# A mixture-of-experts layer in float32 on one core: the last expert's result is merged with its rows on chip instead of being added to them in memory

## The chip, the core and the metric

The kernel runs on one core of a Trainium2 chip. The metric is the time of one execution on the device, in microseconds (us); lower is better. Five engines work beside each other and wait for one another by semaphores: PE (matrix products; its weight loads are listed as PEld), DVE (vector), ACT (scalar), POOL (GpSimd) and SP (which here only issues DMAs). Each engine takes its instructions strictly in the order of its own program.

## What is computed

One layer of a diffusion backbone for 128 prompt rows and 512 sample rows of 1024 channels: a token-mixing part, then a mixture of 16 experts, then a norm of every row. Prompt and sample rows are routed apart; each expert takes its best 16 prompt rows and 64 sample rows, 80 in all, no row twice within one expert:

```python
cap = EC_CAPACITY * n // N_EXPERTS                 # 16 of 128, 64 of 512
g, idx = lax.top_k(jnp.swapaxes(affin, 1, 2), cap)
xe = jax.vmap(lambda xb, ib: xb[ib])(v, idx)
hdn = jax.nn.silu(jnp.einsum('becd,edf->becf', xe, w_e1)) * jnp.einsum('becd,edf->becf', xe, w_e3)
ye = jnp.einsum('becf,efd->becd', hdn, w_e2) * g[..., None].astype(v.dtype)
out = jax.vmap(lambda ib, yb: jnp.zeros((n, D), yb.dtype).at[ib.reshape(-1)].add(yb.reshape(-1, D)))(idx, ye)
...
x = x + g2 * out                                   # in trunk_layer
y_prompt, y_sample = rmsnorm(x, final_norm_g)      # in reference: the final norm of every row
```

All of it is float32. An expert's weights are 24 MB.

## The kernel before

The order of work on each engine is written out by hand. Up to about 685 us the kernel does token mixing and routing; at its end the 640 rows `x` lie in memory in `acc_dram` and their normed form in `xn_dram`, and the table `idx_t` holds in column e the 80 row numbers of expert e (partitions 0 to 63: sample rows, numbered from 128; 64 to 79: prompt rows).

Then come the 16 experts. The weights of one arrive in twelve chunks of 2 MB, issued by SP (L533 in the loop, L507 for the last expert) into six slots of the buffer `ring`; chunk m goes to slot m mod 6, and the issue waits until the products with the slot's old content are done. A chunk is worked in two halves ("units"): ACT rounds it to a high part `w_hi` (L880), DVE takes the rest (L1307, `ring_lo`, written over the slot), and PE multiplies 80 rows by the parts in 24 products of 80x512 (L1649). Chunks 0 to 7 give the hidden rows, chunks 8 to 11 the output in PSUM. Between chunks 7 and 9 PE turns the hidden rows (L1633) and also the rows of the **next** expert (`turn_xe`, L1627), for which POOL has gathered them by their numbers (L603), DVE modulates them (L1297, L1300), ACT rounds (`hi_xe`, L885) and DVE takes the rest (L1313).

When chunk 11's product is done, DVE multiplies the sums by the gates and `g2` into the tile `ye` (`output`, L1331), and POOL adds the 80 rows of `ye` to `acc_dram` with an indirect DMA that accumulates in memory (L618). PE, POOL and the others run the last expert like the rest, as pass 15 of their loops (ACT, DVE and SP have it written out behind a loop of 15). So a 17th gather, turn, modulation and rounding is done whose result nobody uses.

After the last expert: SP waits for the 16th scatter and loads the 640 rows back from `acc_dram` in five tiles of 128x1024 (`xr`, L539). For each tile ACT squares and sums (L929) and takes a root (L932), DVE scales the sum (L941), takes the reciprocal (L1371) and multiplies the tile by it and by the norm's weights (L1373), and SP stores it to the output (L542):

```python
eng.wait_ge(scattered, 16 * E)                     # SP, before L539
...
eng.wait_ge(fin_loaded[t], 16)                     # ACT, before the Square of tile t
...
eng.scalar_tensor_tensor(out=xr[:, n, :], in0=xr[:, n, :], scalar=rstat[:, 3, n:t], in1=gf,
                         op0=ALU.mult, op1=ALU.mult).then_inc(out_ready, 1)
```

Of the kernel before, what the change touches and what calls it, by code (L numbers as in the profile page):

```python
# [16 lines left out]
P = 128  # L17
D = 1024
KD = D // P
NP, NS = 128, 512  # L20
# [8 lines left out]
E = 16  # L29
# [80 lines left out]
def trunk_layer(nc, a):  # L110
# [18 lines left out]
    with ExitStack() as ctx:  # L129
# [47 lines left out]
        idx_s = sb("idx_s", [CAP, 1], U32)  # L177
        ps = ctx.enter_context(nc.psum_tensor("ps", [P, 8, 512], F32))
# [78 lines left out]
        hs = cu_f[0:CAP, 0:FF]  # L257
        gf = cu_f[:, 2 * D:3 * D]
# [122 lines left out]
        fin_loaded = [sem(f"fin_loaded{t}") for t in range(NT)]  # L381
# [58 lines left out]
        def _(eng):  # L440
# [96 lines left out]
            eng.wait_ge(scattered, 16 * E)  # L537
            for t in range(NT):
                eng.dma_start(xr[:, t, :], acc_dram[P * t:P * t + P, :]).then_inc(fin_loaded[t], 16)  # L539
            for t in range(NT):  # L540
                eng.wait_ge(out_ready, t + 1)
                eng.dma_start(a["y_prompt"][0] if t == 0 else a["y_sample"][0].rearrange("(t p) d -> t p d", p=P)[t - 1],  # L542
                              xr[:, t, :]).then_inc(out_stored, 16)
            eng.wait_ge(out_stored, 16 * NT)
            eng.wait_ge(state_stored, 16)

        @block.gpsimd
        def _(eng):
# [62 lines left out]
            with eng.Fori(0, E) as i:  # L611
                eng.wait_ge(xe_turned, i + 1)
                eng.wait_ge(xe_loaded, i * 16 + 16)
                gather(i + 1)
                step.did(eng.tensor_copy(idx_s[:, :], idx_t[:, bass.ds(i, 1)]))
                step.wait()
                eng.wait_ge(ye_ready, i + 1)
                eng.indirect_dma_start(out=acc_dram, out_offset=bass.IndirectOffsetOnAxis(ap=idx_s[:, 0:1], axis=0),  # L618
                                       in_=ye, in_offset=None, compute_op=ALU.add).then_inc(scattered, 16)
                step.restart()  # L620
                eng.wait_ge(scattered, i * 16 + 16)

        @block.scalar
        def _(eng):
# [272 lines left out]
            def act_expert(i, final):  # L897
                for m in range(2, 12):
                    hi_piece(i, m, (i, m - 2))
                    if m == 3:  # L900
                        swish(i, 0)
                    if m == 7:
                        swish(i, 1)
                        hi_h(i, 0)
                    if m == 10:
                        hi_h(i, 1)
                hi_xe(i + 2)
                if not final:
                    for m in range(2):
                        hi_piece(i + 1, m, (i, m + 10))  # L910
# [13 lines left out]
            for t in range(NT + 1):  # L924
                if t < NT:
                    eng.wait_ge(fin_loaded[t], 16)
                    if t >= 2:
                        eng.wait_ge(fin_ssq, t - 1)
                    eng.activation(xn1[:, t % 2, :], xr[:, t, :], ACT.Square, accum_out=rstat[:, 0, t:t + 1]).then_inc(fin_ssq, 1)  # L929
                if t:  # L930
                    eng.wait_ge(fin_ms, t)
                    eng.activation(rstat[:, 2, t - 1:t], rstat[:, 1, t - 1:t], ACT.Sqrt).then_inc(fin_root, 1)  # L932

        @block.vector
        def _(eng):
# [399 lines left out]
            def dve_expert(i, final):  # L1335
                for m in range(2, 12):
# [7 lines left out]
                    if m == 10:  # L1344
                        split_h(i, 1)
                        modulate_xe(i + 2)
                split_xe(i + 2)
                if not final:
                    for m in range(2):
                        split_piece(i + 1, m)  # L1350
                output(i)
                step.restart()

            split_piece(0, 0)
# [10 lines left out]
            for t in range(NT + 1):  # L1365
                if t < NT:
                    inverse_root(fin_ssq, t + 1, fin_ms, fin_root, t, t + 1)
                if t:
# [4 lines left out]
                    eng.scalar_tensor_tensor(out=xr[:, n, :], in0=xr[:, n, :], scalar=rstat[:, 3, n:t], in1=gf,  # L1373
                                             op0=ALU.mult, op1=ALU.mult).then_inc(out_ready, 1)

        @block.tensor
        def _(eng):
# [262 lines left out]
            with eng.Fori(0, E) as i:  # L1640
# [33 lines left out]
                turn_xe(i + 2)  # L1674
# [3 lines left out]
                hidden_product(11)  # L1678

# [26 lines left out]
```

## Time and profile before

| | |
|---|---|
| time, median of 3 runs | 1800.69 us (1800.22 to 1802.33) |
| the profiled execution's own time | 1802.36 us |
| its span, first to last instruction | 1800.6 us |
| busy: PE, DVE, ACT, POOL | 93%, 78%, 61%, 15% of the span |
| granted TensorE clock, mean | 0.966 |
| read from HBM | 478.91 MB |

The span is what the rows below are counted in; a row's time is from the span's start. A busy share is an average over the whole execution and says nothing of its end. The end must be read in the chain of waits, which goes back from the last instruction to what released it, and in the timelines of the engines beside it. "x72" means that a row merges 72 instructions.

### The profile page before, as it was taken

Reading aid. Unit: us, or ns where it says so; the run is one execution under the profiler, and the core shown is the slowest. Engines: PE = TensorE matmul, PEld = TensorE weight load, DVE = VectorE, ACT = ScalarE, POOL = GpSimd, SP = SyncE. Lnnn points to the kernel's source line nnn. Section 1 sums busy time; section 2 is a strip of 40 time slices with the busy share of each in tenths; the row PEclk is TensorE's granted clock in tenths of the full one; section 3 lists DMA queues with packets and bytes.
Section 4 is the critical chain, followed back from the end, with each engine's and each line's share of the span. In section 5 each row is a group of like instructions: output and inputs, shape, how many; then the busy total and the mean of one; then the engine's idle time right before and its main releaser. Section 6 shows DMA issues by size and latency. Waiting matters only on the chain.

```text
span 1800.6 us, 21011 instructions
## 1 busy us (share of the span) xinstructions
PE 1669.5 (93%) x7966; PEld 1176.8 (65%) x7966; DVE 1399.4 (78%) x1308; ACT 1101.8 (61%) x859; POOL 275.3 (15%) x119
## 2 busy tenths in 40 slices
PE   4698889999999938999999999999999999999994
PEld 0298779778888725666666666666666666666662
DVE  0429999974334567988989989989989989989985
ACT  3325544542522335777777777777777777777773
POOL 2003435510000000002011012022022022022020
PEclk8799999999999968999999999999999999999997
DMA  9821111121325286999999999999999999999983
GB/s 389 312 67 57 39 61 40 50 68 59 96 71 165 104 338 237 362 391 366 378 390 373 376 390 359 389 386 367 386 389 362 383 387 371 381 390 370 379 337 124
DMA packets 142558, 492.49 MB, mean 274 GB/s; under 512 B 11257, under 2 KB 23705, under 8 KB 139456
## 3 DMA queue, kind: packets, MB, share of 16 engines
q1 hardware_dynamic: 137280, 475.75, 70.2%
q0 software_dynamic: 3776, 11.09, 2.8%
q10 hardware_dynamic: 1472, 5.25, 0.8%
q8 instruction: 18, 0.29, 0.1%
q14 instruction: 12, 0.10, 0.0%
HBM read 478.91 MB, written 13.16 MB: 273 GB/s over the span
## 4 chain that ended last, share of the span: by engine, by line
PE 81%; DVE 11%; DMA 5%; issue 1%; ACT 1%; SPq 0%; POOL 0%; DVEq 0%; another core or an unknown queue 0%; ACTq 0%; POOLq 0%
PE ps L1649 59%; PE ps L1493 12%; DVE ring L1076 5%; DMA ring<-in_w_mod 3%; PE ps L1455 2%; PE ps L1555 2%; PE ps L1573 1%; DVE ring L1104 1%; PE ps L1633 1%; DVE a_lo L1010 1%; PE ps L1390 1%; PE ps L1470 1%; DVE ring L1051 1%; PE ps L1627 1%; PE ps L1542 0%
## 5 line engine op out<-in xcount | busy, mean ns | idle before, releaser
L1307 DVE TENSOR_TENSOR ring_lo<-ring,w_hi 128x2048 fp32r<-128x2048 f32 x384 | 872.2, 2289 | 109.6 <-ACT w_hi L880 109.6
L880 ACT ACTIVATE w_hi<-ring 128x2048 fp32r<-128x2048 f32 x384 | 734.9, 1919 | 260.5 <-PE ps L1649 260.4
L1649 PE MATMUL ps<-w_hi,xe_hi 128*80 128x512 f32 x1024 | 402.9, 393 | 3.6 <-DVE xe_lo L1313 3.6
L1649 PE MATMUL ps<-ring_lo,xe_hi 128*80 128x512 f32 x1024 | 402.6, 393 | 0.0
L1649 PE MATMUL ps<-w_hi,xe_lo 128*80 128x512 f32 x1024 | 400.7, 391 | 0.0
L1649 PEld LDWEIGHTS ps<-w_hi,xe_hi 128*80 128x80 f32 x1024 | 151.8, 148 | 87.9 <-issue 4.3
L1649 PEld LDWEIGHTS ps<-w_hi,xe_lo 128*80 128x80 f32 x1024 | 151.7, 148 | 84.2 <-issue 0.5
L618 POOL DMA_INDIRECT acc_dram<-ya,idx_s x16 | 75.3, 4709 | 849.3 <-remote 849.3
L1649 PEld LDWEIGHTS ps<-ring_lo,xe_hi 128*80 128x80 f32 x1024 | 151.7, 148 | 81.0 <-issue 0.5
L1649 PE MATMUL ps<-w_hi,h_hi 128*80 128x512 f32 x512 | 203.1, 397 | 0.0
L1649 PE MATMUL ps<-ring_lo,h_hi 128*80 128x512 f32 x512 | 201.2, 393 | 0.0
L1649 PE MATMUL ps<-w_hi,h_lo 128*80 128x512 f32 x512 | 201.1, 393 | 0.0
L1455 PE MATMUL ps<-u_hi,a_hi 128*128 128x320 f32 x384 | 121.0, 315 | 7.7 <-ACT ring L735 4.1
L1076 DVE SCALAR_TENSOR_TENSOR ring<-ring,cur 128x113 f32<-128x113 f32 (+21 forms) x352 | 122.0, 425 | 0.0
L1455 PE MATMUL ps<-u_hi,a_lo 128*128 128x320 f32 x384 | 120.4, 314 | 0.0
L1455 PE MATMUL ps<-u_lo,a_hi 128*128 128x320 f32 x384 | 120.2, 313 | 0.0
L1026 DVE TENSOR_TENSOR b_lo<-ring,b_hi 128x1024 fp32r<-128x1024 f32 x40 | 49.8, 1256 | 84.1 <-ACT b_hi L697 83.8
L1649 PEld LDWEIGHTS ps<-w_hi,h_lo 128*80 128x80 f32 x512 | 75.8, 148 | 43.7
L697 ACT ACTIVATE b_hi<-ring 128x1024 fp32r<-128x1024 f32 x40 | 41.6, 1055 | 99.8 <-DMA ring<-in_w_in 53.1
L1649 PEld LDWEIGHTS ps<-w_hi,h_hi 128*80 128x80 f32 x512 | 75.7, 148 | 41.0
L1649 PEld LDWEIGHTS ps<-ring_lo,h_hi 128*80 128x80 f32 x512 | 75.7, 148 | 40.8
L594 POOL TENSOR_TENSOR ring<-ring 128x644 f32<-128x644 f32 x16 | 70.4, 4426 | 110.8 <-ACT ring L735 110.8
(234 smaller groups left out, 2048.6 us busy)
## 6 DMA issues: line engine op xcount, KB each, us to landing
ring<-in_w_e SPq DMA_DIRECT2D x192, 2048.0 KB, 10.1
ring<-in_w_mod SPq DMA_DIRECT2D x24, 1024.0 KB, 15.7
ring<-in_w_in SPq DMA_DIRECT2D x12, 1024.0 KB, 5.1
ring<-in_w_in SPq DMA_DIRECT2D x16, 512.0 KB, 3.6
xr<-in_x_sample SPq DMA_DIRECT2D x8, 512.0 KB, 5.8
ring<-in_w_rnn_out SPq DMA_DIRECT2D x8, 512.0 KB, 3.7
ring<-in_w_conv_out SPq DMA_DIRECT2D x8, 512.0 KB, 3.8
ring<-in_w_out SPq DMA_DIRECT2D x8, 512.0 KB, 4.1
```

The costliest lines, as they stand in the source:

```text
L594: eng.tensor_tensor(lr_i[:, t, d, :], lr_i[:, t, d, :], xc[:, t, :], ALU.mult).then_inc(ix_ready, 1)
L618: eng.indirect_dma_start(out=acc_dram, out_offset=bass.IndirectOffsetOnAxis(ap=idx_s[:, 0:1], axis=0), in_=ye, in_offset=None, compute_op= ...
L697: eng.activation(b_hi[q % 4][:, :, :], b_raw[:, q % 4, :, :], ACT.Copy).then_inc(piece_hi, 1)
L880: eng.activation(w_hi[m % 2][:, 2 * half:2 * half + 2, :], chunk(m)[:, 2 * half:2 * half + 2, :], ACT.Copy).then_inc(unit_hi, 1)
L1010: eng.tensor_tensor(a_lo[:, kind, :, :], wa(kind), a_hi[kind % 2][:, :, :].bitcast(F32), ALU.subtract)\
L1026: eng.tensor_tensor(b_lo[:, q % 4, :, :], b_raw[:, q % 4, :, :], b_hi[q % 4][:, :, :].bitcast(F32), ALU.subtract)\
L1076: ins = eng.scalar_tensor_tensor(out=cv[:, t, lo:hi], in0=glu[:, t, lo + s:hi + s], scalar=cur[:, G_CDW + k, t:t + 1], in1=cv[:, t, lo:hi] ...
L1307: eng.tensor_tensor(w_lo(m)[:, 2 * half:2 * half + 2, :], w, w_hi[m % 2][:, 2 * half:2 * half + 2, :].bitcast(F32), ALU.subtract)\
L1455: ins = eng.matmul(ps[:, b + h, 0:HALF], w[:, k, :], x[:, k, HALF * h:HALF * h + HALF], start=k == 0 and part == 0, stop=k == KD - 1 and p ...
L1493: ins = eng.matmul(ps[:, tile_bank(NT * g + t), :], x[:, k, P * t:P * t + P], w, start=k == 0 and n == 0, stop=k == KD - 1 and n == 2)
L1555: ins = eng.matmul(ps[:, tile_bank(NT * 8 + t), :], x[:, k, P * t:P * t + P], w, start=k == 0 and n == 0, stop=k == KD - 1 and n == 2)
L1649: ins = eng.matmul(ps[0:CAP, bank + b, :], x[:, k0 + kk, :], w[:, kk, 512 * b:512 * b + 512], start=first and kk == 0 and n == 0, stop=las ...
```

## The change

1. **The last expert's rows are left out of memory's sum.** POOL's loop is one pass shorter. After it, POOL gathers the 80 rows of expert 15 from `acc_dram` (where the first 15 experts are added up) into `xe`, which is free then. When the expert's `ye` is there, DVE adds `xe` to it; ACT and DVE norm these 80 rows with the same steps as a tile, and POOL writes them to the outputs with two indirect DMAs that don't accumulate: 64 rows to `y_sample`, 16 to `y_prompt`, over what lies there. A small table `idx_out` holds their numbers in each output (one DVE instruction and one small DMA fill it).
2. **The norm of all 640 rows doesn't wait for the last expert.** SP loads the five tiles once 15 scatters have landed and chunks 6 and 7 of the last expert are used up, into `ring` (slots 0 and 1), no longer into `xr`, which still holds `w_hi1`. The squares' unused products go there too. One semaphore counts all five loads, and the first square waits for all of them. The tiles are stored as before. The 80 rows of expert 15 are then stored in an unfinished state, and overwritten: POOL waits for all five stores.
3. **Order.** DVE does the five tiles' norm before `output(15)`. PE's last expert is written out behind a loop of 15. The 17th turn, modulation and rounding are gone.

```diff
@@ buffers @@
+        idx_out = sb("idx_out", [CAP_S, 2], U32)
+        fin = ring[:, 0:NT * D].rearrange("p (t d) -> p t d", t=NT)
+        fin_sq = ring[:, NT * D:(NT + 2) * D].rearrange("p (t d) -> p t d", t=2)
@@ SP @@
                 load_chunk(E - 1, m)
-            eng.wait_ge(scattered, 16 * E)
+            product_done(eng, E - 1, NSLOT)
+            product_done(eng, E - 1, NSLOT + 1)
+            eng.wait_ge(scattered, 16 * (E - 1))
             for t in range(NT):
-                eng.dma_start(xr[:, t, :], acc_dram[P * t:P * t + P, :]).then_inc(fin_loaded[t], 16)
+                eng.dma_start(fin[:, t, :], acc_dram[P * t:P * t + P, :]).then_inc(fin_loaded, 16)
...
             eng.wait_ge(out_stored, 16 * NT)
+            eng.wait_ge(rows_patched, 16 * 2)
@@ POOL @@
-            with eng.Fori(0, E) as i:
+            with eng.Fori(0, E - 1) as i:
...
+            eng.dma_start(idx_out[0:CAP_P, 1:2], idx_t[CAP_S:CAP, E - 1:E]).then_inc(last_prompt_idx, 16)
+            eng.wait_ge(xe_turned, E)
+            eng.indirect_dma_start(out=xe, out_offset=None, in_=acc_dram,
+                                   in_offset=bass.IndirectOffsetOnAxis(ap=idx_t[:, E - 1:E], axis=0)).then_inc(xe_loaded, 16)
+            eng.wait_ge(idx_ready, 4)
+            eng.wait_ge(last_prompt_idx, 16)
+            eng.wait_ge(out_stored, 16 * NT)
+            eng.wait_ge(out_ready, NT + 1)
+            for out, column, lo, hi in ((a["y_sample"][0], 0, 0, CAP_S), (a["y_prompt"][0], 1, CAP_S, CAP)):
+                eng.indirect_dma_start(out=out, out_offset=bass.IndirectOffsetOnAxis(ap=idx_out[0:hi - lo, column:column + 1], axis=0),
+                                       in_=ye[lo:hi, :], in_offset=None).then_inc(rows_patched, 16)
@@ ACT, the last expert and after it @@
-                hi_xe(i + 2)
                 if not final:
+                    hi_xe(i + 2)
...
-                    eng.wait_ge(fin_loaded[t], 16)
+                    eng.wait_ge(fin_loaded, 16 * NT)
...
+            eng.wait_ge(ye_ready, E + 1)
+            eng.wait_ge(out_ready, NT)
+            eng.activation(fin_sq[0:CAP, 1, :], ye, ACT.Square, accum_out=rstat[0:CAP, 0, 0:1]).then_inc(fin_ssq, 1)
+            eng.wait_ge(fin_ms, NT + 1)
+            eng.activation(rstat[0:CAP, 2, 0:1], rstat[0:CAP, 1, 0:1], ACT.Sqrt).then_inc(fin_root, 1)
@@ DVE, the last expert and after it @@
-                        modulate_xe(i + 2)
-                split_xe(i + 2)
+                        if not final:
+                            modulate_xe(i + 2)
                 if not final:
+                    split_xe(i + 2)
                     for m in range(2):
                         split_piece(i + 1, m)
-                output(i)
-                step.restart()
+                    output(i)
+                    step.restart()
+            eng.tensor_scalar(idx_out[:, 0:1], idx_t[0:CAP_S, E - 1:E], float(NP), None, ALU.subtract).then_inc(idx_ready, 1)
...
+            output(E - 1)
+            eng.wait_ge(ye_ready, E)
+            eng.wait_ge(xe_loaded, 16 * (E + 1))
+            eng.tensor_tensor(ye, ye, xe, ALU.add).then_inc(ye_ready, 1)
+            eng.wait_ge(fin_ssq, NT + 1)
+            eng.tensor_scalar(rstat[0:CAP, 1, 0:1], rstat[0:CAP, 0, 0:1], 1.0 / D, EPS, ALU.mult, ALU.add).then_inc(fin_ms, 1)
+            eng.wait_ge(fin_root, NT + 1)
+            step.did(eng.reciprocal(rstat[0:CAP, 3, 0:1], rstat[0:CAP, 2, 0:1]))
+            step.wait()
+            eng.scalar_tensor_tensor(out=ye, in0=ye, scalar=rstat[0:CAP, 3, 0:1], in1=gf[0:CAP, :],
+                                     op0=ALU.mult, op1=ALU.mult).then_inc(out_ready, 1)
@@ PE @@
-            with eng.Fori(0, E) as i:
+            def expert(i, final):
...
-                turn_xe(i + 2)
+                if not final:
+                    turn_xe(i + 2)
...
+            with eng.Fori(0, E - 1) as i:
+                expert(i, False)
+            expert(E - 1, True)
```

How the order of instructions moves, at two places. First the end of DVE's program (L1297, L1300 and L1313 are the unused modulation and rest, L1331 is `output`, L941/L1371/L1373 one tile's norm). Before:

```order
L1297 TENSOR_TENSOR ya<-ps,ln_sq 128x640 [waits xe_turned]
L1300 TENSOR_TENSOR ya<-ya,ln_sq 128x640 [waits dve_step]
L1307 TENSOR_TENSOR ring_lo<-ring,w_hi_69 128x2048 [waits unit_hi] x2
L1313 TENSOR_TENSOR xe_lo<-ya,xe_hi 128x640 [waits xe_hi_ready]
L1331 SCALAR_TENSOR_TENSOR ya<-ps,gate_t,ya 80x1024 [waits unit_used]
L88 ISA [waits dve_step]
L941 TENSOR_SCALAR rstat<-rstat 128x1 [waits fin_ssq,gf_loaded]
L941 TENSOR_SCALAR rstat<-rstat 128x1 [waits fin_ssq]
L1371 RECIPROCAL rstat<-rstat 128x1 [waits fin_root]
L1373 SCALAR_TENSOR_TENSOR xr<-xr,rstat,cu 128x1024 [waits dve_step]
...
L1371 RECIPROCAL rstat<-rstat 128x1 [waits fin_root]
L1373 SCALAR_TENSOR_TENSOR xr<-xr,rstat,cu 128x1024 [waits dve_step]
```

With the change (L1360 is `output`, L970/L1402/L1404 a tile's norm, L1411 to L1417 the work on the 80 rows):

```order
L1336 TENSOR_TENSOR ring_lo<-ring,w_hi_69 128x2048 [waits unit_hi] x2
L970 TENSOR_SCALAR rstat<-rstat 128x1 [waits fin_ssq,gf_loaded]
L970 TENSOR_SCALAR rstat<-rstat 128x1 [waits fin_ssq]
L1402 RECIPROCAL rstat<-rstat 128x1 [waits fin_root]
...
L1402 RECIPROCAL rstat<-rstat 128x1 [waits fin_root]
L1404 SCALAR_TENSOR_TENSOR ring<-ring,rstat,cu 128x1024 [waits dve_step]
L1360 SCALAR_TENSOR_TENSOR ya<-ps,gate_t,ya 80x1024 [waits unit_used]
L1411 TENSOR_TENSOR ya<-ya 80x1024 [waits xe_loaded,ye_ready]
L1413 TENSOR_SCALAR rstat<-rstat 80x1 [waits fin_ssq]
L1415 RECIPROCAL rstat<-rstat 80x1 [waits fin_root]
L1417 SCALAR_TENSOR_TENSOR ya<-ya,rstat,cu 80x1024 [waits dve_step]
```

`output` has moved from ahead of the five tiles' norm to behind it, and four instructions follow it that were not there; the three on the unused rows are gone.

Second the end of POOL's program. Before, with the loop over experts from L611 on (the loop's gather is L603, its accumulating scatter L618):

```order
L613 ISA [waits xe_turned]
L601 ISA [waits xe_loaded]
L601 COPY idx_g<-idx_t 80x1
L603 DMA ya<-xn_dram,idx_g 80x1024 [waits pool_step]
L615 ISA
L615 COPY idx_s<-idx_t 80x1
L618 DMA acc_dram<-ya,idx_s 640x1024 [waits ye_ready,pool_step]
L88 ISA [waits pool_step]
L611 REGISTER_ALU [waits scattered]
L611 COMPARE_AND_BRANCH
```

With the change, what follows the loop (L620 is its branch):

```order
L88 ISA [waits pool_step]
L620 REGISTER_ALU [waits scattered]
L620 COMPARE_AND_BRANCH
L633 DMA idx_out<-idx_t 16x1
L635 DMA ya<-acc_dram,idx_t 80x1024 [waits xe_turned]
L642 DMA out_y_sample<-ya,idx_out 512x1024 [waits out_stored,out_ready,last_prompt_idx,idx_ready]
L642 DMA out_y_prompt<-ya,idx_out 128x1024
```

The loop is the same but has one pass fewer; the 16th scatter into `acc_dram` has become one gather from it and two stores into the outputs, the first of which waits for the five tiles' stores and for the normed 80 rows.

## Rows read from the trace of the kernel before

**Rows 1.** The page, part 4: shares of the chain that ended last, by engine
```profile
PE 81%; DVE 11%; DMA 5%; issue 1%; ACT 1%; SPq 0%; POOL 0%; DVEq 0%; another core or an unknown queue 0%; ACTq 0%; POOLq 0%
```

**Rows 2.** Chain of waits, 1741 to 1801 us: start us, us, what
```profile
1758.44 0.68 PE ps L1633 x8
1759.12 0.56 PE ps L1627 x8
1759.67 16.69 PE ps L1649 x72
...
1776.38 1.29 DVE ya L1331
...
1778.46 5.27 DMA acc_dram<-ya,idx_s
...
1784.13 4.82 DMA xr<-acc_dram
...
1796.21 1.28 DVE xr L1373
```

**Rows 3.** Timeline of ACT, 1755 to 1801 us: start us, us, engine, line, operation [idle before]
```profile
1765.26 1.92 ACT L880 ACTIVATE w_hi<-ring 128x2048 fp32r<-128x2048 f32 x1 [0.81 <-PE ps L1649]
...
1767.83 1.28 ACT L922 ACT_TABLE_LOAD   x1
1769.12 0.21 ACT L922 ACTIVATE rstat<-rstat 128x5 f32<-128x5 f32 x1
1787.72 1.06 ACT L929 ACTIVATE cu<-xr 128x1024 f32<-128x1024 f32 x1 [18.39 <-DMA xr<-acc_dram]
...
1792.77 1.06 ACT L929 ACTIVATE cu<-xr 128x1024 f32<-128x1024 f32 x1
...
1794.74 0.20 ACT L932 ACTIVATE rstat<-rstat 128x1 f32<-128x1 f32 x1 [0.73 <-DVE rstat L941]
```

**Rows 4.** Timeline of DVE, 1738 to 1801 us
```profile
1757.08 1.21 DVE L1319 TENSOR_TENSOR cu<-cu,ps 80x1024 f32<-80x1024 f32 x1
...
1762.63 0.82 DVE L1324 TENSOR_TENSOR h_lo<-ps,h_hi 128x640 fp32r<-128x640 f32 x1
...
1764.96 4.55 DVE L1307 TENSOR_TENSOR ring_lo<-ring,w_hi 128x2048 fp32r<-128x2048 f32 x2
...
1788.97 0.15 DVE L941 TENSOR_SCALAR rstat<-rstat 128x1 f32<-128x1 f32 x1 [11.31 <-ACT cu L929]
...
1790.25 0.16 DVE L1371 RECIPROCAL rstat<-rstat 128x1 f32<-128x1 f32 x1
1790.45 1.28 DVE L1373 SCALAR_TENSOR_TENSOR xr<-xr,rstat,cu 128x1024 f32<-128x1024 f32 x1
```

**Rows 5.** Instructions of line L618 (the accumulating scatter), whole execution
```profile
L618 POOL DMA_INDIRECT acc_dram<-ya,idx_s x16: 1450/4927/4935, 761.3 to 1778.5; - x16
...
DMA to landing us min/median/max: 5.3/10.8/11.9
```

**Rows 6.** Instructions of line L603 (the gather), whole execution
```profile
L603 POOL DMA_INDIRECT ya<-xn_dram,idx_g x17: 936/2700/2734, 674.2 to 1724.7; - x17
...
DMA to landing us min/median/max: 3.9/9.5/10.0
```

**Rows 7.** DMA issues, 1750 to 1801 us: issue, count, KB each, median us to landing
```profile
xr<-acc_dram SPq DMA_DIRECT2D x5, 512.0 KB, 5.6
out_y_sample<-xr SPq DMA_DIRECT2D x4, 512.0 KB, 2.7
```

**Rows 8.** Busy time by stretch: stretch, us, busy of each engine, PEclk, DMA share, GB/s
```profile
690.00:780.00 90.00, 90.00 (x409) 58.30 (x408) 78.15 (x40) 69.34 (x42) 7.50 (x4) 1.00 0.96 353
1750.00:1752.00 2.00, 2.00 (x10) 1.33 (x9) 1.66 (x1) 1.75 (x1) 0.00 (x0) 1.00 0.01 2
```

**Rows 9.** The page, part 3: the queue of PE's code, whole execution
```profile
q8 instruction: 18, 0.29, 0.1%
```

**Rows 10.** DMA queues, 700 to 780 us
```profile
q8 instruction: 2, 0.03, 0.2%
```

More of the change, by code:

```diff
@@ L380, in trunk_layer @@
         gf_loaded = sem("gf_loaded")
-        fin_loaded = [sem(f"fin_loaded{t}") for t in range(NT)]
+        fin_loaded = sem("fin_loaded")
+        last_prompt_idx = sem("last_prompt_idx")
+        rows_patched = sem("rows_patched")
         fin_ssq = sem("fin_ssq")
@@ L542, in _ @@
                 eng.dma_start(a["y_prompt"][0] if t == 0 else a["y_sample"][0].rearrange("(t p) d -> t p d", p=P)[t - 1],
-                              xr[:, t, :]).then_inc(out_stored, 16)
+                              fin[:, t, :]).then_inc(out_stored, 16)
             eng.wait_ge(out_stored, 16 * NT)
+            eng.wait_ge(rows_patched, 16 * 2)
             eng.wait_ge(state_stored, 16)
@@ L925, in _ @@
                 if t < NT:
-                    eng.wait_ge(fin_loaded[t], 16)
+                    eng.wait_ge(fin_loaded, 16 * NT)
                     if t >= 2:
                         eng.wait_ge(fin_ssq, t - 1)
-                    eng.activation(xn1[:, t % 2, :], xr[:, t, :], ACT.Square, accum_out=rstat[:, 0, t:t + 1]).then_inc(fin_ssq, 1)
+                    eng.activation(fin_sq[:, t % 2, :], fin[:, t, :], ACT.Square, accum_out=rstat[:, 0, t:t + 1]).then_inc(fin_ssq, 1)
                 if t:
@@ L1372, in _ @@
                     step.wait()
-                    eng.scalar_tensor_tensor(out=xr[:, n, :], in0=xr[:, n, :], scalar=rstat[:, 3, n:t], in1=gf,
+                    eng.scalar_tensor_tensor(out=fin[:, n, :], in0=fin[:, n, :], scalar=rstat[:, 3, n:t], in1=gf,
                                              op0=ALU.mult, op1=ALU.mult).then_inc(out_ready, 1)
+            output(E - 1)
[9 more added lines that the diff above has]
+                                     op0=ALU.mult, op1=ALU.mult).then_inc(out_ready, 1)
         @block.tensor
```

## The prediction

> **What bounds the kernel now.** I read the page's shares of the chain first, then the chain's end, then the timelines of ACT and DVE beside it, and last the DMA views. The chain lies on PE for 81% of the span [rows 1]. Its last piece shows what follows PE: the last products (9 to 11 of expert 15) run from 1759.67 us for 16.69, to 1776.36, and the span ends at 1800.6, so 24.24 us stand behind PE's last product [rows 2]. They are strictly in series: `output` on DVE (1.29), the way to POOL's scatter (from 1777.67 to 1778.46, 0.79), the scatter's landing (5.27), the first tile's loading (4.82 and 0.34 to issue it), five norms, and a store [rows 2]. The reader should see two things beside this. In the last 24 us of PE's work the DMA queues are empty: in 1750 to 1752 us their share is 0.01, where it was 0.96 over 690 to 780 us [rows 8]. And ACT has nothing to do from 1769.33 until 1787.72, DVE from 1769.51 on only the unused rows' rest and `output` [rows 3, 4]. So there is room for the five tiles' norm under PE's products, if the data are there.
>
> **What is removed in front.** PE loses the 17th turn, 0.56 us on the chain [rows 2]: products 9 to 11 start at 1759.12 and, at 16.69 for 72 matmuls, end at 1775.81. Product 10 starts about a third of 16.69 later, at 1764.7, and needs the rest of the hidden rows, which DVE has at 1762.63 + 0.82 = 1763.45 [rows 4]; ACT's and DVE's work ahead of that is not moved, so PE doesn't wait. The rest of chunk 11 is ready by 1769.5 at the latest [rows 4], and its products start near 1770.2. PE's last expert is the same products in straight code; I cost that at nothing (a rival below).
>
> **The loads.** SP issues them when product 7 is done: products 8 and 7 lie before 1758.44, 5.56 each (a third of 16.69), so at 1752.9. The queues are free then [rows 8]. Before, five loads issued from 1783.75 (1784.13 less 0.34 and 0.04) had landed when the fifth Square began at 1792.77 [rows 2, 3], so within 9.0 us, median 5.6 each [rows 7]. Now all have landed by 1762, and the single semaphore costs nothing, since ACT comes to them later. POOL's gather of the 80 rows follows the 15th scatter, early in expert 15, and is needed only at its end; even the slowest gather landed in 10.0 [rows 6]. The index table's instruction and DMA lie under the first gather and under expert 15.
>
> **The five norms.** ACT's last rounding of a weight chunk follows product 9: it ran from 1765.26 for 1.92, and now starts 0.56 earlier, at 1764.70, and ends at 1766.62. The rounding of the unused rows is gone; the table load (1.28) and the small root (0.21) follow, and the first Square starts at about 1768.17 [rows 3]. From the first Square to the end of the fifth product on DVE it was 1787.72 to 1797.49, or 9.77 us [rows 2, 3], paced by DVE. DVE is done with chunk 11 by about 1769.0 (its pair ended at 1769.51 [rows 4], behind work now gone), just before it gets the first sum at 1769.4. So the five tiles are normed at **1777.94**. That is 2.1 us after PE's end: `output(15)` is queued behind the tiles on DVE, and this, no longer PE, sets the end. The last tile's store takes 2.7 [rows 7] and lands at 1780.7, before POOL could want it.
>
> **The 80 rows.** All in series:
> - `output`: 0.02 + 1.29 [rows 2], to 1779.25.
> - The sum with `xe`: no row shows it, the nearest is the 80x1024 product of two tensors, 1.21 [rows 4]; with 0.04 to start, to 1780.50.
> - Square: from its start to DVE's small scaling it was 1787.72 to 1788.97, 1.25 [rows 3, 4], to 1781.75.
> - Scaling 0.15, root 0.20, reciprocal 0.16 [rows 3, 4], with the handovers about 0.6, to 1782.35.
> - Product with the weights: 1.28 [rows 4], to 1783.63.
> - The way to POOL: 0.79, as for the scatter, to 1784.42.
> - Two indirect stores. Nothing like them is in the trace. POOL's time for an 80-row scatter was 1.45 on the quiet chip, for a gather 0.94 [rows 5, 6]. I take 1.45 for the first and 0.3 between them (bounds: 0.94 and 0; 1.45 and 0.79). So the second starts at 1786.2 (1785.4 to 1786.7).
> - Landing, from the second's start: bounds 2.7 (a plain store of 512 KB, [rows 7]) and 5.27 (the accumulating scatter, [rows 2]). I take 3.9, the quickest gather [rows 6], because it is indirect and doesn't accumulate: 1790.1.
> - From the last landing to the span's end it was 1800.6 less (1797.49 + 2.7), about 0.35: **1790.4**.
>
> DMA: Bandwidth & Descriptors of the Trainium skill, section Anatomy of one DMA, gives 2.0 us plus the bytes at 436 GB/s for one DMA of this path. For the 64 KB of prompt rows that is an estimate of 2.15 us; by it the span would end at 1788.7.
>
> **The sum.** 1800.6 - 1790.4 = 10.2 us less. The profiled execution's own time was 1802.36, its span 1800.6; it lay 1.67 above the median of 1800.69. Against the median: 1800.69 - 10.2 = **1790.5 us**. With the bounds of the stores the span ends between 1788.4 and 1792.3, and the time lies between 1788.5 and 1792.4. The 24.24 us behind PE become 14.6: the accumulating scatter (5.27), the reload (4.82) and the series of five norms go; 2.1 us of waiting for DVE's norms, a sum, a second norm and two stores come.
>
> **Rivals.**
> - *The stores cost what the scatters cost in the loop.* There one took 4.93 us on POOL and 10.8 to land [rows 5]. Two in a row would start their second at 1784.42 + 4.93 = 1789.35, land at 1800.2, and the span would end at 1800.5: no change. Against it: the same instruction took 1.45 and 5.27 once DVE and the queues were quiet, and they are quiet here. It decides where POOL's 4.93 comes from the instruction and not from the company. 0.02.
> - *The norms are not hidden.* If the loads are late, or ACT starts its Squares only when PE ends, the change doesn't do what it says. Squares from 1775.81 on, 7.64 later than forecast, give 1798.1 on the span, 1798.2 in time: within 0.2% of before. For it: the first Square waits for all five loads. Against it: they have 6 us in hand. A smaller form, with the tiles' norm stretched by two to six us because it runs beside the products and stores, gives 1793 to 1797. 0.02 for the whole, 0.07 for the smaller form.
> - *PE waits for its code (the slower side).* The code had 2142 matmuls in 18 packets of the code's queue [rows 9], so about 119 to a packet; written out, the last expert adds 304, two or three packets, which must come while the weights fill the queues. A transfer begun there landed after 10.8 us at the median [rows 5]. If none were fetched ahead, one wait of 10.8 would eat the gain, and two give 1790.5 + 21.6 = 1812.1, slower. It decides from one unhidden packet on. Against it: in 700 to 780 us, when PE first goes through the experts' code, two such packets came [rows 10] with the DMA share at 0.96, and PE was busy in 90.00 of 90 us [rows 8]. The same should hold here. Slower 0.03, and 0.01 for a single packet that leaves it level.
>   Runtime: NRT & Kernel Launch of the Trainium skill, section Instruction fetch mechanics, says that straight code streams in mostly hidden while a taken branch to code outside the window costs a fetch; by it the change is free on this count, and rows 8 and 10 agree for the first pass.
> - *The stores are cheaper still.* Both land as quickly as a plain store: 1788.5. It is inside the range.
>
> **How the numbers follow.** Forecast with its bounds 0.85; smaller gain 0.07; no change 0.05 (0.02 + 0.02 + 0.01); slower 0.03. A measurement of this kernel can tell about 0.2%, or 3.6 us, from no change: faster means under 1797.1. The smaller form counts as faster: 0.92, 0.05, 0.03. The range goes from 1787.5, a microsecond under the lower bound since the runs before spread over 2 us, to 1794.5, which takes in the milder part of the smaller form.
>
> **What would show it.** Right: five loads issued near 1752.9 and landed by 1762; the first Square near 1768.2; PE's last product near 1775.8 without a gap at expert 15; the fifth tile done near 1777.9, and DVE's `output` behind it, so that the chain's end leads over ACT and DVE and touches PE only at product 9; POOL's first store near 1784.4; the end near 1790.4. Wrong: a gap in PE after 1708 us (code); a Square later than 1770; POOL busy for more than 1.5 us with one store, or more than 5.3 us from the last issue to landing; or a wait of POOL for the five tiles' stores instead of the normed rows.

## The result, and the profile after

| | before | changed |
|---|---|---|
| time, median of 6 runs | 1801.24 us (1800.01 to 1802.33) | 1793.18 us (1791.81 to 1795.61) |
| the profiled execution's own time, its span | 1802.36, 1800.6 | 1793.08, 1791.3 |
| from PE's last product to the span's end | 24.24 us | 15.04 us |
| packets of the code's queue | 18 | 21 |

The ratio is 0.9956, with an interval of 0.9943 to 0.9969: the change is worth 0.44%, 8.1 us. The forecast was 1790.5 in a range of 1787.5 to 1794.5, 10.2 us below the 1800.69 that the kernel before then had. The two profiled executions differ by 9.3 us.

The chain of waits of the changed kernel from product 9 on (start us, us, what) stands beside [rows 2]. It leaves PE after product 9 and comes back to it nowhere:

```profile
1758.89 0.68 PE ps L1677 x8
1759.57 5.57 PE ps L1694 x24
...
1765.16 1.92 ACT w_hi L902
...
1767.10 1.28 ACT L944
...
1771.00 1.29 DVE ring L1404
...
1776.76 0.04 DVE ring L1404
...
1777.96 1.28 DVE ya L1360
...
1779.27 1.23 DVE ya L1411
...
1780.52 1.16 ACT ring L959 x2
...
1782.32 1.29 DVE ya L1417
...
1784.46 0.93 POOL out_y_sample L642
1785.38 1.16 POOLq L129
```

Products 9 to 11 start at 1759.57 and, at the 16.69 us of [rows 2], end at 1776.26; the last matmul on record ends at 1776.24. That is 0.45 later than forecast: the turn's 0.56 is gone, but the same place was reached 0.45 later in this execution, already at 1758.89. DVE's fifth product of a tile begins at 1776.76, after PE's end, and `output` is queued behind it, as forecast.

SP's queue and the landings answer to [rows 7] (the DMA issues from 1700 us on: KB each, median us to landing):

```profile
1753.40 2.54 SPq L547 DMA_DIRECT2D ring<-acc_dram  x5
1772.32 0.34 SPq L550 DMA_DIRECT2D out_y_prompt<-ring  x1
```

```profile
ring<-acc_dram SPq DMA_DIRECT2D x5, 512.0 KB, 6.0
out_y_sample<-ring SPq DMA_DIRECT2D x4, 512.0 KB, 2.7
...
out_y_sample<-ya,idx_out POOLq DMA_INDIRECT x1, 3.2
out_y_prompt<-ya,idx_out POOLq DMA_INDIRECT x1, 2.8
```

The loads are issued at 1753.40, right behind product 7, and nothing waits for them. The two indirect stores land 3.2 and 2.8 us after their start. POOL's timeline, and the instructions of line L129, in which every engine's program ends (queue, instruction, duration in ns, start):

```profile
1784.46 0.93 POOL L642 DMA_INDIRECT out_y_sample<-ya,idx_out  x1 [56.78 <-DVE ya L1417]
1785.69 0.85 POOL L642 DMA_INDIRECT out_y_prompt<-ya,idx_out  x1 [0.30 <-issue]
```

```profile
L129 POOLq DRAIN  x1: 6295/6295/6295, 1784.7 to 1784.7; - x1
...
L129 SPq DRAIN  x1: 13/13/13, 1788.7 to 1788.7; - x1
L129 SPq EVENT_SEMAPHORE  x1: 17/17/17, 1791.2 to 1791.2; - x1
```

The second store lands at 1785.69 + 2.8 = 1788.5, and SP is through with its waits at 1788.7. But the program ends at 1791.2, with POOL's DRAIN, which runs for 6.3 us from 1784.7. Before, POOL's DRAIN was over long before SP came to its end:

```profile
L129 POOLq DRAIN  x1: 4317/4317/4317, 1783.9 to 1783.9; - x1
...
L129 SPq DRAIN  x1: 13/13/13, 1800.3 to 1800.3; - x1
L129 SPq EVENT_SEMAPHORE  x1: 17/17/17, 1800.5 to 1800.5; - x1
```

### The profile page after: what moved, and what is told of

Its sections match the earlier page's. It is cut to its first block, busy times and chain, and to the rows that moved or that the text cites. A ratio compares the mean times of both kernels' runs of the same rounds, so it can differ in the third digit from the quotient of the medians.

```text
span 1791.3 us, 20982 instructions
## 1 busy us (share of the span) xinstructions
PE 1670.5 (93%) x7958; PEld 1176.3 (66%) x7958; DVE 1400.6 (78%) x1310; ACT 1101.8 (62%) x861; POOL 264.0 (15%) x119
## 4 chain that ended last, share of the span: by engine, by line
PE 81%; DVE 11%; DMA 4%; issue 2%; ACT 1%; POOL 0%; SPq 0%; DVEq 0%; POOLq 0%; ACTq 0%
PE ps L1694 59%; PE ps L1537 12%; DVE ring L1105 5%; DMA ring<-in_w_mod 3%; PE ps L1499 2%; PE ps L1599 2%; PE ps L1617 1%; DVE ring L1133 1%; PE ps L1677 1%; DVE a_lo L1039 1%; PE ps L1434 1%; PE ps L1514 1%; DVE ring L1080 1%; PE ps L1671 1%; PE ps L1586 0%
## 5 line engine op out<-in xcount | busy, mean ns | idle before, releaser
L603 POOL TENSOR_TENSOR ring<-ring 128x644 f32<-128x644 f32 x16 | 70.3, 4423 | 109.8 <-ACT ring L757 109.8
```

What stands on the lines that cost most here:

```text
L603: eng.tensor_tensor(lr_i[:, t, d, :], lr_i[:, t, d, :], xc[:, t, :], ALU.mult).then_inc(ix_ready, 1)
```

## The experiments

The spans of one kernel differ from execution to execution by a few us, and most of it arises before the last expert: PE's last product ended between 1774.8 and 1778.8 in the profiles below. So I count from there (product 9's start plus 16.69) to the span's end. The changed kernel, profiled a second time, gives 14.96 where it gave 15.04. e4 to e9 and e11 were executed once each, so they are read from this count alone; ratios with an interval stand only for e0, e1, e2, e3 and e10.

| kernel | last product ends | span | from there |
|---|---|---|---|
| before | 1776.36 | 1800.6 | 24.24 |
| changed | 1776.26 | 1791.3 | 15.04 |
| changed again (e0) | 1777.64 | 1792.6 | 14.96 |
| e1 loads late | 1778.63 | 1810.2 | 31.57 |
| e8 output before the norms | 1775.60 | 1796.5 | 20.90 |
| e9 PE's last expert in the loop | 1775.34 | 1790.4 | 15.06 |
| e4 POOL waits for the landing | 1778.72 | 1795.9 | 17.18 |
| e5 one store | 1775.16 | 1789.0 | 13.84 |
| e6 plain store by SP | 1776.54 | 1787.0 | 10.46 |
| e7 DVE busy beside the stores | 1778.76 | 1796.2 | 17.44 |
| e11 fifth tile last | 1778.35 | 1792.9 | 14.55 |
| e2 root table early | 1775.77 | 1789.7 | 13.93 |
| e3 and norm taken apart | 1775.20 | 1788.6 | 13.40 |
| e10 and index instruction later | 1774.83 | 1788.2 | 13.37 |

**The control.**

> The changed kernel itself, beside the others on the same chip, to compare with: 8 us less than the kernel before, time near 1793, span 1790 to 1792.

Median 1794.47 of 5 runs (1791.77 to 1795.19), ratio 0.9958 (0.9945 to 0.9972), as the first time; the span, 1792.6, lies just over what I expected.

**e1: the loads after the last product.**

```diff
-            product_done(eng, E - 1, NSLOT)
-            product_done(eng, E - 1, NSLOT + 1)
+            product_done(eng, E - 1, 11)
```

> The changed kernel, but SP issues the five loads only after the last expert's last product (near 1776.3 us) instead of after its product 7. The merge on chip stays, the hiding under PE's products goes. If the gain comes from the hiding alone: the fifth load lands near 1785.5, the first Square starts there (it waits for all five), the fifth tile is done 9.5 us later at 1795, the 80 rows and the stores follow in the 13.3 us that they took in the changed kernel: span near 1808, time near 1810, slower than the kernel before. If the merge itself saved time on its own, it would stay under 1801. If the loads were not what the norms wait for, the span would not move from 1791.3.

Median 1810.82, ratio 1.0051 (1.0036 to 1.0066), slower than before. The chain:

```profile
1761.95 16.68 PE ps L1693 x72
...
1778.65 0.34 SPq L546
...
1780.46 6.93 DMA ring<-acc_dram
...
1787.41 1.47 ACT ring L950 x3
```

ACT starts 8.8 us behind PE's end, and 31.57 us follow where 31.7 were expected. So in this arrangement all of the gain is that loads and norms lie under PE's products, and without that the change costs 7.3 us. The merge on chip is what lets them lie there; that follows from the program, no run loads early without it.

**e8: `output` ahead of the norms on DVE.**

```diff
             eng.wait_ge(gf_loaded, 16)
+            eng.wait_ge(scattered, 16 * (E - 1))
+            output(E - 1)
             for t in range(NT + 1):
...
-            output(E - 1)
             eng.wait_ge(ye_ready, E)
```

> The changed kernel, but DVE does output of the last expert ahead of the five tiles' norm, where it stood before the change; everything else as changed. DVE works in order, so its first scaling of a tile waits for PE's last product (near 1776.3) and output (1.28). If the order on DVE carries the hiding: the five tiles take from 1777.6 to about 1785.0, the sum follows, and the rest is as it was (12.1 us from the sum's start to the span's end): the span ends 20.8 us behind PE's last product instead of 15.0, near 1797. If DVE's queue was not what holds the norms, it stays at 15.0.

20.90 against 20.8. DVE's queue order carries 5.9 us of the 9.2: an engine that works in order must not be given the instruction that waits for PE ahead of work that doesn't.

**e9: PE's last expert back in the loop.**

```diff
-            with eng.Fori(0, E - 1) as i:
+            with eng.Fori(0, E) as i:
                 expert(i, False)
-            expert(E - 1, True)
```
(with the turn kept in every pass)

> The changed kernel, but PE runs the last expert as the 16th pass of its loop again, with the turn of 8 unused tiles (0.56 us) between products 8 and 9; its code is not written out. If the written-out code costs nothing: the code's queue goes back to 18 packets, the 72 products of chunks 9 to 11 take 16.69 us as they did written out, and only the turn's 0.56 comes back ahead of them. If the written-out code did cost PE time, the products from 1708 us on would run shorter here than in the changed kernel, which had no gap over 0.3 us there but at the turns.

The code's queue has 18 packets again, the turn's 0.55 us is back, and product 9 takes the same 5.57 us in both:

```profile
1758.10 0.55 PE ps L1671 x8
1758.65 5.57 PE ps L1694 x24
```

15.06 against 15.04. In the 58 us from 1700 to 1758, too, PE is busy for 58.00 in the kernel before, in the changed one and here. The three more packets cost PE nothing; that rival is out.

**e4 to e6: what lies between the landing and the end.** The forecast had 0.35 us there, the profile shows 2.8. Three kernels ask what POOL's DRAIN follows.

e4:
```diff
                                        in_=ye[lo:hi, :], in_offset=None).then_inc(rows_patched, 16)
+            eng.wait_ge(rows_patched, 16 * 2)
```

> The changed kernel, but POOL itself also waits for both indirect stores to have landed before its program ends. In the changed kernel the stores landed at 1788.5 and POOL's DRAIN ended at 1791.0, with which the span ends. Theory A, the drain costs about 4.4 us from the moment POOL has no other work: it starts at 1788.5 and the span grows by 1.9, to 1793.2 (counted from the last product's end: 16.9 instead of 15.0). Theory B, the drain waits for the transfers and ends 2.5 us behind their landing whatever POOL does before: the span stays at 15.0 behind the last product.

```profile
L129 POOLq DRAIN  x1: 4480/4480/4480, 1791.2 to 1791.2; - x1
L129 SPq DRAIN  x1: 13/13/13, 1791.2 to 1791.2; - x1
```

POOL is free at 1791.2, when the stores have landed, and its DRAIN still takes 4.5 us. Theory A: 17.18 (16.9 expected), not 15.0.

e5, without the store of the 16 prompt rows (SP waits for one landing, not two):
```diff
-            for out, column, lo, hi in ((a["y_sample"][0], 0, 0, CAP_S), (a["y_prompt"][0], 1, CAP_S, CAP)):
+            for out, column, lo, hi in ((a["y_sample"][0], 0, 0, CAP_S),):
```

> The changed kernel without the second indirect store: the 16 prompt rows of the last expert are not written over in y_prompt, so this leaves out part of the result. The second store was busy on POOL 0.85 us behind a gap of 0.30. Theory A (drain a fixed time behind POOL's last work): the span ends 1.15 us earlier, 13.8 behind the last product instead of 15.0. Theory B (a fixed time behind the last landing): the first store landed 3.2 after its start instead of 1.23 + 2.8, so 0.8 earlier, 14.2 behind the last product.

13.84 against 13.8 by theory A and 14.2 by B. The DRAIN (5.67 us from 1783.1) ends 4.5 us behind the store's end on POOL, at 1784.28.

e6, with no store on POOL: SP writes the 80 rows to working memory instead, and its lines are these (POOL's two waits and its loop of stores are taken out):
```diff
+            eng.wait_ge(out_ready, NT + 1)
+            eng.dma_start(acc_dram[0:CAP, :], ye).then_inc(rows_patched, 16)
+            eng.wait_ge(rows_patched, 16)
```

> The changed kernel, but the 80 finished rows are stored by SP with one plain DMA to the first 80 rows of the working memory, and POOL issues nothing after its gather: the last expert's rows are not written over in the outputs, so this leaves out part of the result. It prices the indirect path as a whole. If POOL's drain sets the end of the changed kernel: SP's store is issued 0.02 us after DVE's last product, lands 2.7 later, and the span ends 0.35 behind that, 7.3 + 3.1 = 10.4 us behind the last product of PE instead of 15.0. If the end of the program costs 2.5 us behind any last transfer, 12.6.

```profile
L129 POOLq DRAIN  x1: 5116/5116/5116, 1731.8 to 1731.8; - x1
...
L129 SPq DRAIN  x1: 13/13/13, 1786.7 to 1786.7; - x1
L129 SPq EVENT_SEMAPHORE  x1: 17/17/17, 1786.9 to 1786.9; - x1
```

10.46 against 10.4. POOL's DRAIN still takes 5.1 us, but lies at 1731.8, under PE's products. So the indirect path costs 4.6 us more than a plain store by SP. About half of it lies behind the landing (2.8 us to the end, some 0.5 in e6), where only POOL's DRAIN still runs; the rest is POOL's later start, the second store and the slower landing. What the DRAIN does in its 4.5 us no run shows.

**e7: DVE busy beside the stores.** Four subtractions whose result isn't used:
```diff
+            eng.wait_ge(out_ready, NT + 1)
+            for n in range(4):
+                step.did(eng.tensor_tensor(w_lo(11)[:, 0:2, :], w_hi[0][:, 0:2, :].bitcast(F32), w_hi[1][:, 0:2, :].bitcast(F32), ALU.subtract))
+                step.wait()
```

> The changed kernel, and DVE does four more 128x2048 subtractions of some 2.3 us each, whose result is not used, while POOL issues the two indirect stores. This asks the rival's question. If POOL's 4.9 us for an indirect DMA in the expert loop came from DVE's company, the two stores take about 4.9 us each instead of 0.93 and 0.85 and the span grows by 4 to 8 us. If it came from the full DMA queues or from the accumulation, they stay at about 0.9 and the span stays at 15.0 us behind PE's last product, since the extra DVE work ends at about 1793.3 less the start at 1783.7, that is within a us or two of the end.

```profile
1786.96 2.27 POOL L642 DMA_INDIRECT out_y_sample<-ya,idx_out  x1 [56.78 <-DVE ya L1417]
1789.54 1.95 POOL L642 DMA_INDIRECT out_y_prompt<-ya,idx_out  x1 [0.30 <-issue]
```

```profile
L129 POOLq DRAIN  x1: 8742/8742/8742, 1787.2 to 1787.2; - x1
```

Neither expectation holds whole. DVE's company makes the stores 2.27 and 1.95 us long instead of 0.93 and 0.85. The DRAIN's 8.7 instead of 6.3 is the same 2.4 us over again: it begins beside the stores and ends 4.45 us behind the second one's end on POOL (1791.49), as it did in the changed kernel (4.46 behind 1786.54). The stores are not made 4.9 long; the loop's scatter is one of 80 rows that accumulates, among full queues, and these runs don't part the two. The end is 2.4 us later. The rival's mechanism is thus real, and absent at this place because DVE has nothing left to do. SBUF — State Buffer of the Trainium skill, section SBUF: two separate sides, says that DVE and GpSimd share a pair of ports, and that a DMA issued by GpSimd can't write its descriptors while DVE runs an instruction in a two-port mode; a DVE instruction with two inputs in SBUF, as the subtractions are, takes the pair only against a GpSimd operation that reads SBUF. The trace agrees in that only POOL's side grew (0.93 to 2.27 us), while DVE's subtractions took 2.30 us, 2.29 in the experts; which of the page's two cases this is, no run here shows.

**e11: the fifth tile behind the sum.** `output` and the sum go ahead of the fifth tile's product in DVE's order, and ACT's last Square waits for four tiles, not five:

```diff
             for t in range(NT + 1):
+                if t == NT:
+                    output(E - 1)
+                    eng.wait_ge(ye_ready, E)
+                    eng.wait_ge(xe_loaded, 16 * (E + 1))
+                    eng.tensor_tensor(ye, ye, xe, ALU.add).then_inc(ye_ready, 1)
```

> The changed kernel, but on DVE output and the sum of the 80 rows go ahead of the fifth tile's product, which then lies in the time in which DVE waits for ACT's Square. Output starts when the fourth tile is done, near 1776.65 instead of 1777.96, so DVE's part is 1.0 us earlier. But the fifth tile is done near 1780.6 and its store lands near 1783.3, and POOL waits for all five stores: it would start at about 1783.5 plus 0.8 instead of 1784.46. I expect a gain of 0.1 to 0.5 us, 14.5 to 14.9 us from PE's last product to the span's end; if POOL's wait for the stores were not what holds it, 14.0.

14.55. As expected a new wait takes most of the gain: the chain now leads over the fifth tile's store.

```profile
1781.29 1.29 DVE ring L1409
...
1782.60 2.62 DMA out_y_sample<-ring
...
1786.12 0.93 POOL out_y_sample L642
```

**e2, e3 and e10: a version that beats both.** The small root that loads ACT's table stood behind the last weight rounding, on the chain (1.28 us). e2 moves it into the last expert, behind the second swish:

```diff
                         swish(i, 1)
                         hi_h(i, 0)
+                        if final:
+                            eng.activation(rstat[:, 2, :], rstat[:, 1, :], ACT.Sqrt)
...
-            eng.activation(rstat[:, 2, :], rstat[:, 1, :], ACT.Sqrt)
```

> The changed kernel, but the small root that brings ACT's table in is done right after the last expert's last swish (near 1746 us) instead of behind the last weight rounding. ACT has about 0.9 us of idle time before each rounding there, and the table load is 1.28. If DVE's norm of the tiles, queued ahead of output, sets the end: the first Square starts near 1767.1 instead of 1768.5, DVE's first product of a tile at about 1770.0 instead of 1771.0 (DVE is busy with the last chunk until 1769.4), the fifth tile is done near 1777.0 and the span is 1.0 us shorter, 1790.3. If PE's end set it, the span would stay at 1791.3. If the table load delayed the weight roundings, PE would show a gap near 1753 and the span would grow by up to 1.3.

```profile
1744.75 1.28 ACT L928 ACT_TABLE_LOAD   x1
...
1766.50 1.04 ACT L951 ACTIVATE ring<-ring 128x1024 f32<-128x1024 f32 x1
```

13.93, 1.1 less. DVE now does the first small scaling right behind its last work on chunk 11, and `output` starts 0.6 us behind PE's end instead of 1.7. Median 1791.37, ratio 0.9945 (0.9931 to 0.9958).

e3 also multiplies by the norm's weights while ACT squares:

```diff
+            eng.wait_ge(ye_ready, E + 1)
+            step.did(eng.tensor_tensor(xe, ye, gf[0:CAP, :], ALU.mult))
...
-            eng.scalar_tensor_tensor(out=ye, in0=ye, scalar=rstat[0:CAP, 3, 0:1], in1=gf[0:CAP, :],
-                                     op0=ALU.mult, op1=ALU.mult).then_inc(out_ready, 1)
+            eng.tensor_scalar(ye, xe, rstat[0:CAP, 3, 0:1], None, ALU.mult).then_inc(out_ready, 1)
```

> As the run before it, and the norm of the 80 rows is taken apart: DVE multiplies them by the norm's weights while ACT squares them, and only a scaling by the root's reciprocal stays behind the root. The product of 1.29 us behind the root becomes a scaling of 0.6 to 1.2; the product moved ahead ends about 0.1 after the Square. The chain is shorter by 0.1 to 0.6 more, span 1789.7 to 1790.2, if the 80 rows are in series to the end; no shorter if POOL waited for the five tiles' stores (they land near 1780.8, before the rows are ready at about 1782.2, so I expect it doesn't).

The scaling behind the root takes 0.75 us where the product took 1.28: 13.40. The span, 1788.6, is below what I gave, since PE's last product ended early in this execution. Median 1790.43, ratio 0.9943 (0.9929 to 0.9956). The intervals of e2 and e3 overlap the changed kernel's (0.9945 to 0.9972 in the same series, e0); that they are better rests on the 13.93 and 13.40 against 15.04 and 14.96.

e10 asks a question that came up only in the changed profiles. POOL's first rows in the expert part, of the kernel before and of the changed one:

```profile
671.56 2.31 POOL L601 COPY idx_g<-idx_t 80x1 uint32<-80x1 uint32 x1 [306.01 <-DVE gate_t L1289]
674.16 2.73 POOL L603 DMA_INDIRECT ya<-xn_dram,idx_g  x1 [0.29 <-POOL idx_g L601]
```

```profile
670.48 4.57 POOL L610 COPY idx_g<-idx_t 80x1 uint32<-80x1 uint32 x1 [305.71 <-DVE gate_t L1318]
675.34 1.01 POOL L612 DMA_INDIRECT ya<-xn_dram,idx_g  x1 [0.30 <-POOL idx_g L610]
```

The copy that the first gather waits for took 2.31 us before, and 4.57 with the change; PE's first turn started 8.42 us after the copy's start before (at 679.98) and 8.89 after it now (at 679.37). DVE beside it, with the change:

```profile
670.45 0.15 DVE L1384 TENSOR_SCALAR idx_out<-idx_t 64x1 uint32<-64x1 uint32 x1
670.52 4.47 DVE L1336 TENSOR_TENSOR ring_lo<-ring,w_hi 128x2048 fp32r<-128x2048 f32 x2
```

The first of them is new, the one that fills `idx_out`, which I had costed at nothing. e10 is e3 with it moved behind the subtractions:

```diff
-            eng.tensor_scalar(idx_out[:, 0:1], idx_t[0:CAP_S, E - 1:E], float(NP), None, ALU.subtract).then_inc(idx_ready, 1)
             split_piece(0, 0)
...
             split_piece(0, 1)
+            eng.tensor_scalar(idx_out[:, 0:1], idx_t[0:CAP_S, E - 1:E], float(NP), None, ALU.subtract).then_inc(idx_ready, 1)
```

> The run with the early root table and the norm taken apart, and the DVE instruction that fills the small index table is moved from ahead of the first expert's weight subtractions to behind them. Before the change POOL's copy of the first gather's index column took 2.31 us and the first turn of PE started 8.42 after the copy's start; in all changed kernels so far the copy took 4.57 and the turn started 8.89 after it. If the new DVE instruction ahead of the subtractions is the cause (it shifts when they begin against POOL's copy), the copy goes back to about 2.3 and the way to the first turn to 8.4: 0.5 us less. If the cause is something else, both stay at 4.57 and 8.9. Behind PE's last product the span stays at 13.4 us as in the run with the norm taken apart. Time near 1790.

```profile
670.88 2.31 POOL L610 COPY idx_g<-idx_t 80x1 uint32<-80x1 uint32 x1 [305.77 <-DVE gate_t L1318]
673.48 2.74 POOL L612 DMA_INDIRECT ya<-xn_dram,idx_g  x1 [0.30 <-POOL idx_g L610]
```

The copy is back at 2.31, and the turn starts at 679.23, 8.35 after the copy's start; in the other changed kernels it was 8.89 to 9.16. So the instruction cost some 0.5 us, by the way in which POOL's copy and DVE's two subtractions of 2.3 us met. Before and in e10 the copy started 0.03 us behind the first subtraction and ended with it; with the change it started 0.04 ahead of it and ended with the second. A wait for the port that POOL and DVE share (SBUF — State Buffer of the Trainium skill, section SBUF: two separate sides) would explain these lengths. The section's rule that the first to start keeps the pair doesn't fit them: by these starts the copy was first where it took 4.57. No run here shows the port. Median 1790.25 us, ratio 0.9935 (0.9921 to 0.9948) against a kernel before of 1802.36 in that series: the lowest ratio here, level with e3's within the intervals. Its interval and the changed kernel's overlap a little; that it is better rests on the profiles' 13.37 against 15.04.

## Why the prediction was right, and where it wasn't

**The mechanism was right.** Loads near 1752.9 (measured 1753.40), the first Square near 1768.2 (1768.50), the fifth tile done near 1777.9 (1778.04), `output` behind it on DVE, PE's end at 1775.8 (1776.26) and not on the chain any more, POOL's first store near 1784.4 (1784.46). The series from the fifth tile's end to the first store was given as 6.48 us and took 6.42. e1 and e8 show that both halves of the reason hold: without the early loads 31.57 us follow PE's end, without DVE's new order 20.90.

**The stores and the end were right only in sum.** Four terms missed:
- Between PE's end and POOL's first store I had 8.61, measured 8.20: from the first Square the five tiles took 9.54 us instead of 9.77, and ACT came to it 0.1 sooner.
- The first store and the gap behind it: 1.78 (1.45 and 0.3, rounded up), measured 1.23 (0.93 and 0.30). I took the price of an accumulating scatter; the gather's row, 0.94, was the right one.
- The landing: 3.9 from the quickest gather, measured 2.8. The plain store's row, 2.7, was the right one. DMA: Bandwidth & Descriptors of the Trainium skill (section Anatomy of one DMA) had given 2.15 for it; the measurement decides, and the page's figure was nearer than my choice.
- **From the last landing to the end: 0.35, measured 2.8.** This is the step that failed in kind. I took it from a kernel whose last DMAs are SP's. Where POOL issues the last one, the program waits for POOL's DRAIN, 4.5 us behind its last work (e4, e5, e6). The row stood in the profile of the kernel before: POOL's DRAIN of 4.3 us from 1783.9, hidden then because SP was busy until 1800.2. I didn't look for it.

The terms cancel, and that is luck: 14.6 us were given behind PE's last product, 15.04 came, with 2.45 too little at the end and 2.06 too much ahead of it.

**The time was 2.7 us higher than forecast, though the span was only 0.9.** 0.45 of that is where PE's end lay. The way from POOL's first copy to PE's turn was 0.47 longer, which is the index instruction (e10): it "lies under the first gather" only if nothing on POOL meets it. The first 144 matmuls took 1.00 longer (the last section), and POOL's copy had started 1.08 earlier. 0.4 is the sum above. The rest is the step to the median: I took off the 1.67 us by which the profiled execution before lay above its median. The changed kernel's profiled execution lay at its median (1793.08 against 1793.18). One execution's distance from the median does not carry over to another kernel.

**The rivals.** The stores did not cost what the scatters cost in the loop, but e7 shows that part of that price is DVE's company. The norms were hidden: from the first issue to ACT's start the five loads took 8.8 us in e1, which from 1753.40 gives an estimate of 1762.2, and the first Square began 6 us later. PE waited for no code: its last products are as long in e9 with 18 packets as in the changed kernel with 21, and PE was busy throughout from 1700 to 1758 in both. Runtime: NRT & Kernel Launch of the Trainium skill, section Instruction fetch mechanics, has straight code stream in mostly hidden; here it was hidden wholly, as far as the rows show.

## What to carry to other kernels

When a last result has to be combined with stored data, ask which of the two is late: combine the late part on chip and let everything that doesn't depend on it run under the last products, but check each in-order queue for an instruction that waits for the late part ahead of work that doesn't (here 5.9 of 9.2 us hung on DVE's order). Look up each engine's own end of program (the DRAIN row) before making it the last one to work: POOL's ended 4.5 us behind its last DMA's end on POOL here, 2.5 behind the landing, while SP's took 0.01. Where two engines share a moment, a new instruction of 0.15 us can cost three times its length by changing which of them starts first.

## What the runs showed that I had not expected

POOL's DRAIN, above. Where POOL first waited for the landing of its last DMA, it took 4.3 us (before) and 4.5 (e4) from the end of that wait; where POOL didn't wait, it ended 4.5 us behind the last store's end on POOL (changed, e5), beside a busy DVE too (e7). Under the products, with nothing of POOL's left, it took 5.1 (e6).

The start of the experts is uneven. PE's granted clock is at 0.50, that is 1.2 GHz, when the first expert's products begin after a stretch with little for PE, and rises to 1.00 (2.4 GHz) a few us later, not always after the same time. From 640 to 684 us PE was busy for 9.12 of 44 us before and for 8.04 in the changed kernel. Kernel before, then changed (stretch, us, busy of PE, PEld, DVE, ACT, POOL, PEclk, DMA share, GB/s):

```profile
686.00:688.00 2.00, 2.00 (x6) 1.12 (x6) 2.00 (x2) 0.00 (x0) 0.00 (x0) 0.50 0.00 0
688.00:690.00 2.00, 2.00 (x9) 1.23 (x8) 1.13 (x1) 0.30 (x1) 0.00 (x0) 0.80 0.00 0
690.00:692.00 2.00, 2.00 (x10) 1.29 (x9) 0.36 (x1) 1.61 (x1) 0.00 (x0) 1.00 0.00 0
```

```profile
686.00:688.00 2.00, 2.00 (x6) 1.24 (x5) 2.00 (x2) 0.00 (x0) 0.00 (x0) 0.50 0.00 0
688.00:690.00 2.00, 2.00 (x6) 1.11 (x6) 0.53 (x1) 0.30 (x1) 0.00 (x0) 0.50 0.00 0
690.00:692.00 2.00, 2.00 (x10) 1.24 (x9) 0.36 (x1) 1.61 (x1) 0.00 (x0) 0.91 0.00 0
```

The matmuls start 0.43 us apart at the lower level and 0.23 at the upper; 9 lie before the rise in the kernel before (until 688.78), 14 in the changed one (until 690.31), which is the 1.0 us between them: the first 144 matmuls (chunks 0 to 5) took 35.12 us before, 36.12 in the changed kernel's profile, 36.07 in its second, and between 34.54 and 36.07 in kernels with the same code at that place. So up to 1.6 us of a single execution's time are this, more than several terms of the sum; it is why the experiments are read from PE's last product on.
